# Router's products by tokens beside the output product, choice over all 32 experts at once, offsets by triangular products, weights behind the indices

## What is computed

```python
h = h + m @ w_o[i]
n2 = rms_norm(h, g_ffn[i]).reshape(b * s, d)
...
gl = (xn @ w_group).astype(jnp.float32) + b_group
grp = jnp.argmax(gl, axis=-1)
p_grp = jnp.take_along_axis(jax.nn.softmax(gl, axis=-1), grp[:, None], axis=1)
el = ((xn @ w_router).astype(jnp.float32) + b_router).reshape(t, N_GROUPS, EXPERTS_PER_GROUP)
el = jnp.take_along_axis(el, grp[:, None, None], axis=1)[:, 0]
top_l, top_i = lax.top_k(el, TOP_K)
wgt = (p_grp * jax.nn.softmax(top_l, axis=-1)).reshape(-1)
eid = (grp[:, None] * EXPERTS_PER_GROUP + top_i).reshape(-1).astype(jnp.int32)
...
hdn = jax.nn.silu(xb @ w1[e]) * (xb @ w3[e])
return hdn @ w2[e]
```

## Time and profile before

| what | value |
|---|---|
| median of 3 runs | 2106.74 us (2106.37 to 2107.16) |
| profiled execution | 2106.93 us |
| its span | 2105.1 us |
| granted TensorE clock, mean | 0.953 of full speed |
| TensorE busy | 1922.1 us (91%) |
| VectorE busy | 977.8 us (46%) |
| ScalarE busy | 649.4 us (31%) |
| POOL busy | 182.2 us (9%) |
| HBM read | 349.38 MB |

### The profile page before, as it was taken

The page is one execution under the profiler, slowest core; times in us unless marked ns, Lnnn a source line. Parts: engine busy times, 40 slices in busy tenths (PEclk is TensorE's granted clock), DMA queues, the critical chain, the costliest instruction groups (busy, mean ns, idle before and its releaser), DMA issues.

```text
span 2105.1 us, 33205 instructions
## 1 busy us (share of the span) xinstructions
PE 1922.1 (91%) x14316; PEld 1629.6 (77%) x14316; DVE 977.8 (46%) x1769; ACT 649.4 (31%) x1210; POOL 182.2 (9%) x170
## 2 busy tenths in 40 slices
PE   6899999949999999989799999997898879999997
PEld 4676688736666666658689999997766779999996
DVE  4755434342333223336974322347765574323355
ACT  5334323211100100026443222234455543222242
POOL 0012100000000000000300000014122410000012
PEclk9999999959999999989899999998999979999998
DMA  4221242639999999962202232243211233332342
GB/s 166 71 80 68 76 170 90 259 123 424 426 427 427 425 427 426 427 280 67 73 24 91 91 101 81 91 132 112 88 51 41 94 103 124 101 101 81 101 140 81
DMA packets 58087, 355.78 MB, mean 169 GB/s; under 512 B 6304, under 2 KB 8992, under 8 KB 45648
## 3 DMA queue, kind: packets, MB, share of 16 engines
q1 hardware_dynamic: 53968, 340.02, 42.3%
q0 software_dynamic: 3504, 12.73, 1.6%
q10 hardware_dynamic: 464, 0.85, 0.1%
HBM read 349.38 MB, written 4.19 MB: 168 GB/s over the span
## 4 chain that ended last, share of the span: by engine, by line
PE 72%; DVE 11%; DMA 9%; ACT 4%; issue 2%; POOL 1%; SPq 0%; ACTq 0%; DVEq 0%; POOLq 0%
PE bank L427 51%; DMA e<-in_we 9%; PE bank L609 7%; PE bank L631 4%; PE bank L473 1%; ACT SS L2440 1%; DVE wlo L1108 1%; PE bank L642 1%; PE bank L758 1%; PE bank L643 1%; DVE scr L1266 1%; DVE ztmp L1710 1%; POOL zacc L2545 1%; DVE SS L1850 1%; DVE sm L1857 1%
## 5 line engine op out<-in xcount | busy, mean ns | idle before, releaser
L427 PE MATMUL bank<-nhi,whi 128*128 128x256 f32 (+2 forms) x1472 | 424.5, 288 | 3.4 <-DVE nlo L1720 1.9
L427 PE MATMUL bank<-nhi,wlo 128*128 128x256 f32 (+2 forms) x1472 | 420.2, 285 | 0.0
L427 PE MATMUL bank<-nlo,whi 128*128 128x256 f32 (+2 forms) x1472 | 420.0, 285 | 0.0
L1108 DVE TENSOR_TENSOR wlo<-raw,whi 128x1024 fp32r<-128x1024 f32 x243 | 303.8, 1257 | 136.5 <-ACT whi L1964 132.8
L1964 ACT CAST whi<-raw 128x1024 fp32r<-128x1024 f32 x247 | 256.6, 1043 | 130.9 <-PE bank L427 108.6
L427 PEld LDWEIGHTS bank<-nhi,whi 128*128 128x128 f32 x1472 | 279.7, 190 | 8.5 <-DVE nlo L1720 2.5
L427 PEld LDWEIGHTS bank<-nhi,wlo 128*128 128x128 f32 x1472 | 279.0, 190 | 1.5
L427 PEld LDWEIGHTS bank<-nlo,whi 128*128 128x128 f32 x1472 | 279.4, 190 | 0.9
L609 PE MATMUL bank<-e,xT 128*64 128x256 f32 x2048 | 237.2, 385 | 1.0 <-DVE xT L1395 1.0
L609 PEld LDWEIGHTS bank<-e,xT 128*64 128x64 f32 x2048 | 143.2, 138 | 82.9 <-issue 15.0
L427 PE MATMUL bank<-ghi,whi 128*128 128x256 f32 (+1 forms) x704 | 200.8, 285 | 0.0
(11 more groups left out here) (330 smaller groups left out, 2962.6 us busy)
## 6 DMA issues: line engine op xcount, KB each, us to landing
e<-in_we SPq DMA_DIRECT2D x96, 2048.0 KB, 34.9
raw<-in_w_down SPq DMA_DIRECT2D x64, 512.0 KB, 3.3
raw<-in_w_gate SPq DMA_DIRECT2D x48, 512.0 KB, 3.3
raw<-in_w_up SPq DMA_DIRECT2D x48, 512.0 KB, 3.3
raw<-in_w_q SPq DMA_DIRECT2D x12, 512.0 KB, 4.2
B<-in_rel POOLq DMA_DIRECT2D x8, 512.0 KB, 4.0
raw<-in_w_gc SPq DMA_DIRECT2D x8, 512.0 KB, 3.2
raw<-in_w_ga SPq DMA_DIRECT2D x8, 512.0 KB, 4.3
```

Of the source, the lines that this page charges most:

```text
L427: i = e.matmul(o, a, x[:, k0 + k, c0:c1], start=(k == 0 and n == 0), stop=(k == j.K - 1 and n == 2))
L1108: e.tensor_tensor(wlo[wslot(u)][:], raw[u % NRAW][:], whi[wslot(u)][:].bitcast(F32), ALU.subtract).then_inc(*hit("dve_low", ("lo", u)))
```

## The change

The logits are computed with tokens on the output's partitions: hT is the stationary operand, the router's weights move (36 columns). Each eighth k of this is issued between two tiles of the output product (after tile k + 1), the last two behind it; the scaling of the router's weights moves ahead of the output product. ScalarE squares each piece of hT behind its addition, POOL sums the first seven in rb, and two sets of four products with a column of ones give the sums of squares by token. ScalarE then scales the turned pieces straight from PSUM into n2k; the turning order is N2, one piece ahead of the sums and seven behind.

VectorE masks out the 24 experts of other groups and chooses over all 32 at once, so that the masks M of the two choices come directly. TensorE gives counts by expert on partitions, the ranks in four products, and the exclusive and inclusive prefix sums of extra blocks as products with a triangle. Choices are laid out (j i), choice first, instead of (i j). POOL multiplies pa by the token numbers (pat) for the index products; the weight products follow with pa and pw, and pw, the overflow table and the copies stand behind the cast of the indices. The loading of the Silu table is asked for at the end of act_route.

```diff
+                if m:
+                    logits(m - 1)
+
+        def logits(k):
+
+            w.wait_ge(*at("wr g"))
+            w.wait_ge(*at("free", "wo", k, 0))
+            for i in range(4):
+                if k == 0:
+                    take(("lg", i), SIDE)
+                p = e.matmul(bank[BANK["lg", i]][:, 0:36], hT[:, k, MT + i * 128:MT + (i + 1) * 128], wr[:, k, :],
+                             start=(k == 0), stop=(k == 7))
+            p.then_inc(*hit("pe_route", *([("logits",)] if k == 7 else [])))
...
-            for i in range(4):
-                for hf in range(2):
-                    b = take(("n2", i, hf), DENSE)
-                    for k in range(4):
-                        w.wait_ge(*at("free", "wo", 4 * hf + k, 0))
-                        p = e.transpose(b[:, k * 128:(k + 1) * 128],
-                                        hT[:, 4 * hf + k, MT + i * 128:MT + (i + 1) * 128], ident)
-                    p.then_inc(*hit("pe_turn", ("turned n2", i, hf)))
...
-            b = take(("lgT",), SIDE)
-            w.wait_ge(*at("wr g"))
-            for k in range(8):
-                p = e.matmul(b[0:36, :], wr[:, k, :], hT[:, k, MT:L], start=(k == 0), stop=(k == 7))
-            p.then_inc(*hit("pe_route", ("logits",)))
-            b = take(("lg",), SIDE)
-            w.wait_ge(*at("free", "lgT"))
-            for i in range(4):
-                p = e.transpose(b[:, i * 36:(i + 1) * 36], rb[0:36, i * 128:(i + 1) * 128], ident[0:36, 0:36])
-            p.then_inc(*hit("pe_route", ("logits by token",)))
-            b = take(("rk",), SIDE)
...
+            def turn_n2(i, hf):
+                b = take(("n2", i, hf), DENSE)
+                for k in range(4):
+                    w.wait_ge(*at("free", "wo", 4 * hf + k, 0))
+                    p = e.transpose(b[:, k * 128:(k + 1) * 128], hT[:, 4 * hf + k, MT + i * 128:MT + (i + 1) * 128], ident)
+                p.then_inc(*hit("pe_turn", ("turned n2", i, hf)))
+
+            turn_n2(*N2[0])
+            for n, x in enumerate((rb[:, 0:S], sg[:, 1, :])):
+                b = take(("col", "n2", n), DENSE)
+                w.wait_ge(*(at("n2 sq", 7) if n else at("n2 acc", 6)))
+                for i in range(4):
+                    p = e.matmul(b[:, i:i + 1], x[:, i * 128:(i + 1) * 128], ones[:, 0:1], start=True, stop=True)
+                p.then_inc(*hit("pe_route", ("col", "n2", n)))
+                if not n:
+                    logits(7)
+            for x in N2[1:]:
+                turn_n2(*x)
...
+            bc, br, bx = (take((x,), SIDE) for x in ("counts", "ranks", "extras"))
             w.wait_ge(*at("chosen"))
             for i in range(4):
-                for i2 in range(i + 1):
-                    e.matmul(b[:, 32 * i:32 * i + 32], tri if i2 == i else ones, R["Ms"][:, i2, :], start=(i2 == 0),
-                             stop=(i2 == i))
-            for i2 in range(4):
-                p = e.matmul(b[:, 128:160], ones, R["Ms"][:, i2, :], start=(i2 == 0), stop=(i2 == 3))
+                p = e.matmul(bc[0:32, 0:1], R["Ms"][:, i, :], ones[:, 0:1], start=(i == 0), stop=(i == 3))
+            p.then_inc(*hit("pe_route", ("counts",)))
+            e.matmul(br[:, 0:128], tri, Ms, start=True, stop=False)
+            for i in (1, 2, 3):
+                p = e.matmul(br[:, 32 * i:128], ones, Ms[:, 0:128 - 32 * i], start=False, stop=(i == 3))
             p.then_inc(*hit("pe_route", ("ranks",)))
-            w.wait_ge(*at("places"))
-            for n in range(2):
+            e.matmul(bx[:, 0:32], ones[0:1, :], R["c31"][0:1, :], start=True, stop=False)
+            w.wait_ge(*at("extra"))
+            x = R["extra"][0:32, :].to_broadcast([32, 128])
+            e.matmul(bx[:, 0:32], x, tri[0:32, 0:32], start=False, stop=True)
+            e.matmul(bx[:, 32:64], x, tri[0:32, 1:33], start=True, stop=True).then_inc(*hit("pe_route", ("extras",)))
+            for n, (a, q) in enumerate((("pat", "pb"), ("pa", "pw"))):
                 b = take(("by place", n), SIDE)
+                w.wait_ge(*at(a))
+                w.wait_ge(*at(q))
...
+    N2 = [(i + x, hf) for i in (0, 2) for hf in range(2) for x in range(2)]
...
-            w.wait_ge(*at("n2 sq"))
-            dv(e.tensor_tensor, ns[:, 2, 0:4], ns[:, 0, 0:4], ns[:, 1, 0:4], ALU.add)
-            dv(e.tensor_scalar, ns[:, 2, 0:4], ns[:, 2, 0:4], 1.0 / D, EPS, ALU.mult, ALU.add, ev=[("mean", "n2")])
-            root(e, w, ns[:, 3, 0:4], ns[:, 2, 0:4], ns[:, 0, 0:4], "dve_root", "n2")
-            w.wait_ge(*at("logits"))
-            dv(e.tensor_copy, rb[0:36, 0:S], bank[BANK["lgT",]][0:36, :], ev=[("free", "lgT")])
-            w.wait_ge(*at("logits by token"))
-            w.wait_ge(*at("root", "n2"))
-            dv(e.tensor_tensor, lg[:], bk("lg", n=144).rearrange("p (i r) -> p i r", i=4),
-               ns[:, 3, 0:4].unsqueeze(2).to_broadcast([128, 4, 36]), ALU.mult, ev=[("free", "lg")])
...
+            w.wait_ge(*at("col", "n2", 0))
+            e.tensor_scalar(ns[:, 2, :], bk("col", "n2", 0, n=4), 1.0 / D, EPS, ALU.mult, ALU.add).then_inc(
+                *hit("dve_mean", ("free", "col", "n2", 0)))
+            w.wait_ge(*last("dve_mean"))
+            w.wait_ge(*at("col", "n2", 1))
+            e.scalar_tensor_tensor(ns[:, 1, :], bk("col", "n2", 1, n=4), 1.0 / D, ns[:, 2, :], ALU.mult, ALU.add).then_inc(
+                *hit("dve_mean", ("mean", "n2"), ("free", "col", "n2", 1)))
+            root(e, w, ns[:, 0, :], ns[:, 1, :], ns[:, 2, :], "dve_root", "n2")
+            w.wait_ge(*at("logits"))
+            w.wait_ge(*at("root", "n2"))
+                e.scalar_tensor_tensor(lg[:, i, :], bk("lg", i, n=36), ns[:, 0, i:i + 1], row("b_r", 0, 36), ALU.mult,
+                                       ALU.add).then_inc(*hit("dve_route", ("free", "lg", i)))
...
+            def first_of(x, n, m, eq, ix):
+                dv(e.scalar_tensor_tensor, eq, eq, -64.0, iota[:, 0:n].unsqueeze(1).to_broadcast([128, 4, n]), ALU.mult,
+                   ALU.add)
+            es, eq, M, ix = R["es"], R["eq"], R["M"], R["ix"]
+            first_of(gl, 4, R["mg"], R["eqg"], R["ixg"])
+            dv(e.tensor_tensor, R["ne"], R["eqg"], R["ixg"].to_broadcast([128, 4, 4]), ALU.is_gt)
+            for g in range(4):
+                if not g:
+                    w.wait_ge(*last("dve_route"))
+                e.scalar_tensor_tensor(es[:, :, 8 * g:8 * g + 8], R["ne"][:, :, g:g + 1].to_broadcast([128, 4, 8]), -3.0e38,
+                                       el[:, :, 8 * g:8 * g + 8], ALU.mult, ALU.add).then_inc(*hit("dve_route"))
+            for j in range(2):
+                first_of(es, 32, R[f"m{j + 1}"], eq, ix[:, j])
+                dv(e.tensor_tensor, M[:, j], eq, ix[:, j].to_broadcast([128, 4, 32]), ALU.is_equal)
+                if not j:
+                    dv(e.scalar_tensor_tensor, es, M[:, 0], -3.0e38, es, ALU.mult, ALU.add)
+            dv(e.tensor_tensor, R["Ms"], M[:, 0], M[:, 1], ALU.add, ev=[("chosen",)])
+            dv(e.tensor_tensor, R["ge"], gl, R["mg"].to_broadcast([128, 4, 4]), ALU.subtract, ev=[("gl shifted",)])
+            dv(e.tensor_tensor, R["ee"], R["m2"], R["m1"], ALU.subtract, ev=[("l2 shifted",)])
+            w.wait_ge(*at("counts"))
+            dv(e.tensor_tensor, R["big"][0:32, :], i7[0:32, :], bank[BANK["counts",]][0:32, 0:1].to_broadcast([32, 7]), ALU.is_lt,
+               ev=[("free", "counts")])
+            dv(e.tensor_reduce, R["extra"][0:32, :], R["big"][0:32, :], AX.X, ALU.add, ev=[("extra",)])
+            t, r8, o8, ge7, bq, place, blk = (R[x] for x in ("t", "r", "o", "ge7", "bq", "place", "blk"))
+            t8 = t.rearrange("p j i r -> p (j i) r")
+            w.wait_ge(*at("ranks"))
+            dv(e.tensor_tensor, t, M, bk("ranks", n=128).rearrange("p (i r) -> p i r", i=4).unsqueeze(1).to_broadcast(
+                [128, 2, 4, 32]), ALU.mult, ev=[("free", "ranks")])
+            dv(e.tensor_reduce, r8.unsqueeze(2), t8, AX.X, ALU.add)
+            dv(e.tensor_tensor, ge7, r8.unsqueeze(2).to_broadcast([128, 8, 7]), i7.unsqueeze(1).to_broadcast([128, 8, 7]),
+               ALU.is_ge)
+            dv(e.tensor_reduce, bq.unsqueeze(2), ge7, AX.X, ALU.add)
+            dv(e.scalar_tensor_tensor, place, bq, -64.0, r8, ALU.mult, ALU.add)
+            dv(e.tensor_tensor, R["pa"], place.unsqueeze(2).to_broadcast([128, 8, 64]),
+               iota[:, 0:64].unsqueeze(1).to_broadcast([128, 8, 64]), ALU.is_equal, ev=[("pa",)])
+            w.wait_ge(*at("extras"))
+            dv(e.tensor_tensor, t, M, bk("extras", n=32).unsqueeze(1).unsqueeze(1).to_broadcast([128, 2, 4, 32]), ALU.mult)
+            dv(e.tensor_reduce, o8.unsqueeze(2), t8, AX.X, ALU.add)
+            dv(e.tensor_tensor, o8, o8, bq, ALU.add)
+            dv(e.scalar_tensor_tensor, o8, bq, 1.0, o8, ALU.min, ALU.mult)
+            dv(e.scalar_tensor_tensor, blk, ix.rearrange("p j i x -> p (j i x)"), 64.0, o8, ALU.add, ALU.add)
...
```

(51 more changed lines are left out.)

120 lines of the change are left out of this document (32 added, 88 removed), and 4 rows, old and new, of the table k.

## The result

The changed kernel takes 2086.35 us (median; 2084.04 to 2088.48) where the kernel before takes 2106.55 beside it (2106.04 to 2107.16): ratio 0.9904, 95% interval 0.9887 to 0.9921. Its profiled execution lasted 2086.74 us, with a span of 2084.1. The forecast was 2088.5 with a range of 2083.5 to 2094.

What follows compares the result with a forecast made beforehand. It took the router, up to the first expert product, to hold back the expert weight stream. Terms 1.7 - 7.9 - 3.55 - 8.5 = -18.3 us, from 2106.93 (median 2106.74), gave 2088.5 us, range 2083.5 to 2094.

Steps and rivals of the forecast that it cites:

- Logits: Eight logit groups beside the output product, 0.89 us each; six move the last tile's end to 414.4 us.
- Rival (a): Logits in the output product cost double, 7.2 us more, giving 2095.7 us; chance 6 in 100.
- Squares and POOL: Squares of h and POOL's additions of them are hidden beside the output product; 1.3 us if uncovered.
- Norm and choice: VectorE's norm, logits and expert choice take 8.5 us instead of 16.38: -7.9.
- Turnings: Seven leftover turnings for the gathered table, ahead of the counts on TensorE, cost 0 to 0.5 us.
- Counts and ranks: TensorE's count and rank products, at the lower clock, take 2.65 us instead of 6.22: -3.55.
- Places and blocks: VectorE's steps from ranks to index products take 4.45 us instead of 12.96: -8.5.
- Weights behind the indices: Second set of index products ends some 4 us after the cast, hidden behind the gather's over 5 us.
- Cast to first expert product: Gather, turning and scaling after the cast of the indices stay at 8.38 us.
- rival (b): Gather waits for the normed tokens' stores, starting 3 us late if they land at 440.3: 2091.5 us; 6 in 100.
- (c): The weight stream, not the router, sets the end, so the gain is given back: 2106.7 us; 3 in 100.
- (d): TensorE's granted clock does not come back in the expert stage: 2113.4 us at 50 us of low clock; 3 in 100.

Runs made afterwards that it cites:

- Run 1: Changed kernel with forty more chained small VectorE steps (8.0 us) ahead of the cast of the indices; 2098.52 us, ratio 0.9963.
- run 9: Changed kernel with the last two logit groups behind the column sums and spare products in TensorE's router pauses, ninth weight load not held; 2085.94 us.
- run 2: Changed kernel with the first seven logit groups also moved behind the last output tile, none left inside the output product; 2094.05 us, ratio 0.9944.
- Run 8: Kernel before with only the weights' steps, weight mask and overflow table moved behind the block masks or the cast of the indices; 2097.25 us.
- run 5: Changed kernel once more, unaltered, on another chip, to know its scatter; 2085.64 us, ratio 0.9902.
- run 7: Changed kernel with last two logit groups behind the column sums, spare products in TensorE's pauses, ninth load held until the second gather landed; 2082.31 us.
- run 4: Changed kernel with 32 spare 128-column products in TensorE's router pauses, into a bank nobody reads; 2086.47 us, ratio 0.9908.
- run 6: Changed kernel with the ninth weight load held until the second gather has landed; 2086.24 us, ratio 0.9901.
- run 11: Kernel before with only ranks, counts and offsets changed to fewer, one-column and triangular products; 2095.34 us, ratio 0.9949.
- run 12: Changed kernel with last two logit groups behind column sums, spare products in router and tail, ninth load held until the first gather landed; 2080.89 us.
- run 3: Changed kernel with the last two logit groups moved behind both column sums; 2086.67 us, ratio 0.9913.
- run 10: Changed kernel with ten spare 128-column products ahead of the down products of each of the last two expert pairs; 2088.63 us, ratio 0.9919.

## Why the prediction was right, point by point

- **What bounds it.** Right. The first expert product and the stream moved together: -18.97 for the product, -19.9 for the tenth load, -18.16 for the load behind the experts (w_ple_proj at 872.85, 891.01 before). Run 1 put a delay in and got it back one to one in its lower heap. The prediction's own sign, that everything behind the expert stage shifts by what the first expert product shifted, held for these loads within 1.0, but not behind them: the cast of h came 23.0 sooner (922.08, 945.08 before), the end of the span 21.0. Gains and losses of 2 to 3 us in the router can't be followed to the end (run 9).
- **Logits.** Right, at 0.94 a tile (tile spacing 6.38 instead of 5.44) against 0.89. The last addition came at 413.89, forecast 414.4; the 0.5 between them is the earlier start (0.76) less the dearer groups (0.28). Rival (a), double price, is what the row at low clock would have given; run 2 shows it happens there (1.90 a group) and that it doesn't inside the output product (window 370 to 414: clock 1.00). What was not in the forecast: that the place keeps the clock, which is worth 2.5 us up to the cast.
- **Squares and POOL.** Hidden, as said: POOL's addition ended at 410.3, the sum over it began at 414.98.
- **Norm and choice.** 8.53 against 8.5. The spacings taken from the earlier trace rows held to 0.01: 422.34 to 425.58 is ten steps in 3.24.
- **Turnings.** Nothing, out of 0 to 0.5. They ran at 0.20 each (4.68 us for 24), and TensorE still waited 0.93 us for the choice. The clock had fallen to 0.50 at 418 and was back at 1.00 from 425 on, with nothing but turnings on TensorE since 420.74. The rule of the Trainium skill, page "TensorE: Matmul & The Clock Gate", section "Part 4: PE-mode transpose", which the prediction cites, fits neither that rise nor the 32 turnings at 0.14 and 1.00 in the earlier trace rows; the traces decide against it here. No time hangs on it.
- **Counts and ranks.** The term that was mis-sized: -4.79, forecast -3.55. The forecast took the low clock granted in that place before. But now the turnings run just ahead of them and the granted clock was 1.00 from 425 to 428: the four count products took 0.39 in all and the four rank products 1.1, not 0.18 and 0.45 each. It fell again at 428, was 0.50 through TensorE's wait of 3.49 us, and the index products had the low-clock price (3.18), as forecast.
- **Places and blocks.** 4.62 against 4.45. POOL's product took 1.04 (430.16), not 1.27, and was no wait. The two-input VectorE step at 431.09 started 0.03 after the one before it while POOL's row ends at 431.20, so the exclusion that the prediction cites from the Trainium skill, page "SBUF — State Buffer", section "Who interferes with whom", by which it would have waited for that end, cost nothing that these rows show, where 0.5 us was allowed for.
- **Weights behind the indices.** Hidden, as said: the second set ended at 439.66, the turning began at 442.40. Run 8 measured the part alone.
- **Cast to first expert product.** The step that failed: that "the stretch to the first expert product (8.38)" stays, with the remark that nothing of the gain meets a full DMA. The stores landed where the forecast put them (432.22, forecast 432), so rival (b) fell; but their landing releases the ninth load, and this one met the gather. The forecast wrote down both events, the load that "could go" when the stores are out and the gather 5 us later, and looked only at whether the gather waits for the stores. Before, the load was long over by 456. It measured 1.2 us (0.4 in run 5, the same kernel; 2.0 in run 9, against the 8.38). That is its price on the way to the first expert product; what it costs at the end is not shown.
- **Behind the first expert product.** Forecast unchanged, measured -2.03. By the two profiles: 0.44 up to the start of the last-but-one pair's down product, although the first expert's product alone took 0.95 less (8.72 instead of 9.67); 1.16 in that down product (8.81 instead of 9.97); 2.43 in the first dense work behind the stage (15.02 instead of 17.46); and 2.00 lost again from the cast of h to the end (1162.02 instead of 1160.02). These places move from execution to execution (the down product was 7.13 in the changed kernel's other profile), so the -2.03 can't be credited to the change. Rivals (c) and (d) are out: the granted clock was 0.93 from 445 to 470 us and 1.00 from 454 on, with the DMA share at 1.02 there.

So the median is 2.15 us below the forecast. In the profiles the difference lies outside the router, 0.76 ahead of it and 2.03 behind it; in the router +1.2 and -1.2 cancel, which is luck.

## What to carry to other kernels

When a serial stage in front of a saturated stream is shortened, cut the trace at its events and cost each stretch by the spacing of chained steps (0.20 us for a small one, 0.325 for 128 elements here): that gave five of the router's seven terms within 0.4 us. Then list every transfer that the shortened chain now releases or meets, not only those that it waits for. Narrow products did best inside a dense product (run 2): they cost the same there, but in a long run behind it the clock fell, and the products after them took nearly double. And a gain of 2 or 3 us in such a stage has to be looked for at the stage's end as well as at its first product: in run 7 the one showed 2.9 us of the hold and the other 0.2.

## What the runs showed of the hardware that was not expected

- TensorE busy for 8.00 of 8.00 us with f32 products of 36 columns and the turnings and one-column products behind them lost its clock: 0.89 in that window, 0.50 in the next (run 2). With the same products spread through a dense stretch it stood at 1.00 (370 to 414 us). Products of 128 columns in the pauses held 0.93 (run 4) and 1.00 (run 7) from 425 to 437, where the changed kernel has 0.62.
- An f32 product with 128 weight columns and 36 moving ones costs 0.24 us at full clock, one with a single moving column 0.23 (0.95 for four), at low clock 0.48 and 0.46 (1.90 and 1.84 for four): the moving columns hardly show.
- The first gather lands in 4.6 to 4.9 us with no load beside it (before, runs 1, 6, 7, 8, 11, 12) and in 5.4 to 7.8 when a 2 MB load was issued 1.0 to 4.5 us ahead of it (after and runs 3, 4, 5, 9, 10), the longer the younger the load; 5.3 us behind the load's issue it took 4.9, though that load had 3.5 us to go (run 2).
- Spare products are not free where they end late: fourteen of them held TensorE 1.4 us beyond the gather in run 4, 0.4 in run 7; ten cost 2.42 in run 10.
- Executions of one kernel differ by 5 us and more, mostly along with their mean granted clock. One place of it lies over 1100 us behind any change: 1600 to 1640 us had 0.91 in run 7 and 1.00 in run 9, and the way from the expert stage to the end 1161.9 and 1158.8 us.
